# Sublayers begun token tile by token tile, weights in 1024-column units split in place, modulation made one stage ahead, in an eleven-stage transformer kernel

## The reference, cut to what matters

```python
def adaln_sublayer(x, m, f, ln_g, ln_b):          # stages 0 to 5
    shift, scale, gate = m[:, None, 0], m[:, None, 1], m[:, None, 2]
    y = f(x * (1 + scale) + shift)
    return layer_norm(DEEPNORM_ALPHA * x + (1 + gate) * y, ln_g, ln_b)

mod = silu(c) @ mod_w[layer] + mod_b[layer]       # 2 layers x 9 rows of 1024
# stages 0, 2, 3, 5: f = 0.5 * (silu(u @ w_gate) * (u @ w_up)) @ w_down, inner width 2816
# stage 1: sparse attention and a gated delta rule; stage 4: latent attention (MLA)
# stages 6, 8: x + 0.5 * mixer(rms_norm(x)): two softmax branches and a gated linear
#              attention (GLA), joined by gates
# stages 7, 9: x + (conv over tokens of the up product, gated) @ w_down, of rms_norm(x)
```

## Time and profile before

| | before |
|---|---|
| median of 3 runs | 2538.28 us |
| the profiled execution, its own time | 2538.26 us |
| its span | 2536.5 us |
| PE busy | 2260.5 us (89%) |
| DVE, ACT, POOL busy | 1394.2, 1031.8, 292.5 us |
| chain that ended last | PE 77%, DVE 9%, DMA 5%, ACT 4% |
| moved by DMA | 412.79 MB, mean 163 GB/s |
| granted PE clock, mean | 0.915 |

### The profile page before, as it was taken

The page is one execution under the profiler, slowest core; times in us unless marked ns, Lnnn a source line. Parts: engine busy times, 40 slices in busy tenths (PEclk is TensorE's granted clock), DMA queues, the critical chain, the costliest instruction groups (busy, mean ns, idle before and its releaser), DMA issues.

```text
span 2536.5 us, 34860 instructions
## 1 busy us (share of the span) xinstructions
PE 2260.5 (89%) x14352; PEld 1933.7 (76%) x14352; DVE 1394.2 (55%) x2047; ACT 1031.8 (41%) x1725; POOL 292.5 (12%) x414
## 2 busy tenths in 40 slices
PE   5999889979998998788999588987999778897999
PEld 3998778759986996566998566766998667666997
DVE  3545578664455455366454566335665465445664
ACT  1444353333443443264444343342554333343553
POOL 0000200130002002023000222040000121220000
PEclk8999899989999999798999798858999888858999
DMA  9986432459767874625765343303665433303663
GB/s 318 267 237 230 136 113 95 133 159 300 197 225 226 241 223 159 216 76 162 193 194 191 105 134 100 116 17 109 164 185 191 123 126 91 133 10 107 188 184 137
DMA packets 442750, 412.79 MB, mean 163 GB/s; under 512 B 22034, under 2 KB 387814, under 8 KB 442464
## 3 DMA queue, kind: packets, MB, share of 16 engines
q1 hardware_dynamic: 435488, 388.80, 50.8%
q0 software_dynamic: 7104, 21.76, 2.9%
HBM read 407.90 MB, written 2.62 MB: 162 GB/s over the span
## 4 chain that ended last, share of the span: by engine, by line
PE 77%; DVE 9%; DMA 5%; ACT 4%; issue 2%; POOL 2%; SPq 0%; DVEq 0%; ACTq 0%; POOLq 0%
PE ps L170 74%; PE ps L173 3%; DVE arena L179 2%; DMA arena<-in_mod_w 2%; DVE wlo L179 2%; ACT whi L176 2%; ACT arena L176 1%; DMA raw<-in_ffn_w_up 1%; DVE tmp L179 1%; DVE arena L191 1%; DMA raw<-in_mla_w_q_up 1%; POOL arena L221 1%; POOL tmp L179 1%; DVE small L197 1%; DVE ul L179 0%
## 5 line engine op out<-in xcount | busy, mean ns | idle before, releaser
L179 DVE TENSOR_TENSOR wlo<-raw,whi 128x1024 fp32r<-128x1024 f32 (+2 forms) x594 | 728.8, 1231 | 737.3 <-ACT whi L176 736.9
L176 ACT ACTIVATE whi<-raw 128x1024 fp32r<-128x1024 f32 (+2 forms) x594 | 608.3, 1043 | 463.9 <-PE ps L170 408.6
L170 PE MATMUL ps<-uh,whi 128*128 128x256 f32 x2392 | 694.5, 290 | 23.5 <-DVE mb L191 8.1
L170 PE MATMUL ps<-ul,whi 128*128 128x256 f32 x2392 | 685.9, 287 | 0.0
L170 PE MATMUL ps<-uh,wlo 128*128 128x256 f32 x2392 | 685.5, 287 | 0.0
L170 PEld LDWEIGHTS ps<-uh,whi 128*128 128x128 f32 x2392 | 468.9, 196 | 44.7 <-issue 21.1
L170 PEld LDWEIGHTS ps<-ul,whi 128*128 128x128 f32 x2392 | 468.9, 196 | 0.3 <-issue 0.2
L170 PEld LDWEIGHTS ps<-uh,wlo 128*128 128x128 f32 x2392 | 468.3, 196 | 0.0
L170 PE MATMUL ps<-whi,arena_r 128*128 128x512 f32 x1184 | 367.0, 390 | 0.0
L170 PE MATMUL ps<-whi,uh 128*128 128x512 f32 (+3 forms) x594 | 251.3, 423 | 72.6 <-ACT arena L176 28.5
L170 PE MATMUL ps<-arena 128*128 128x128 f32 (+8 forms) x1360 | 262.5, 341 | 28.4 <-DVE tmp L191 10.8
(11 more groups left out here) (179 smaller groups left out, 1794.7 us busy)
## 6 DMA issues: line engine op xcount, KB each, us to landing
arena<-in_mod_w SPq DMA_DIRECT2D x64, 1024.0 KB, 7.1
raw<-in_ffn_w_gate SPq DMA_DIRECT2D x88, 512.0 KB, 6.6
raw<-in_ffn_w_up SPq DMA_DIRECT2D x88, 512.0 KB, 6.9
raw<-in_ffn_w_down SPq DMA_DIRECT2D x44, 1024.0 KB, 5.0
raw<-in_w_in SPq DMA_DIRECT2D x44, 1024.0 KB, 5.2
raw<-in_w_up SPq DMA_DIRECT2D x88, 512.0 KB, 5.1
raw<-in_w_down SPq DMA_DIRECT2D x22, 1024.0 KB, 4.9
raw<-in_hyb_w_in SPq DMA_DIRECT2D x16, 1024.0 KB, 5.3
```

The lines of the kernel that those rows point to most:

```text
L170: return Nothing() if self.raw is None else self.raw.matmul(out, l, r, start=start, stop=stop)
L176: return Nothing() if self.raw is None else self.raw.activation(out, src, func, **kw)
L179: return Nothing() if self.raw is None else self.raw.tensor_tensor(out, a, b, op)
```

## The change

It has five parts. (1) Weights: a ring of eight units of 128 x 1024 (0.5 MB); the low part is written over `raw`, so a place is free only when PE has used the unit (`sp_units` waits for `used`). The low part of `wlo` has no place of its own any more. (2) FFN: PE takes blocks (c, t): 256 columns of gate and 256 of up beside each other, the weights moving with 512 columns and u of one token tile stationary. The result stands with tokens on partitions and is transposed by two matmuls for each block (`pe_ffn_turn`). The first blocks are (0,0), (1,0), (0,1), (1,1). (3) Stages 1, 4, 6 and 8 begin with one or two 512-column products by token tile (`pe_tok_halves`): z in stage 1, c0 in stage 4, gv and t1a in the mixers, which stood later in the stage before. (4) The boundary is done for t = 0 first, in halves of 512 columns, and for t = 1 under the first products of the next stage. (5) Modulation groups belong to the stage ahead: none at the boundary but two products where an FFN follows; twelve in an FFN's blocks, in the rest of stage 1, or between the attention units of stage 4 instead of its projections. `LATE` is 4.

```diff
+def sp_units(sp, M, n=1):
+    for u in range(sp.unit, min(sp.unit + n, len(M.units))):
+        if u >= NUNIT:                      # 8
+            sp.wait_ge(*sp.on("used", u - NUNIT))
...
+def pe_tok_halves(pe, M, jobs, ready, between):
+    for t in range(T):
+        for tag, src, c0, c1, banks, emptied in jobs:
...
+            for uid, v in units[tag]:
+                pe.wait_ge(*pe.on("lo", uid))
+                for i in range(v.hi.shape[1]):
+                    pe.each(*ready(t, k))
...
+        if t == 0:
+            between()                       # transposes u of t = 1
...
+MOD_BLOCKS = (2, 4, 5, 7, 9, 10, 12, 14, 15, 17, 19, 20)
+UNITS_AFTER = [0, 0, 2, 4] + [2] * (2 * NC - 4)
 def pe_ffn(...):
+    for j, (c, t) in enumerate(FFN_ORDER):
+        if j == 2:
+            second_half()
+        if j > 1:
+            pe_mod_sum(pe, M, 3)
...
+        for uid, v in units[c]:
+            pe.wait_ge(*pe.on("lo", uid))
+            for r in range(2):
+                pe.each(*ready(t, k))
+                last = mm3(pe, bank, M.uT[:, k, t * P:(t + 1) * P], v[:, r, :], k == 0, k == KD - 1)
...
+        for i in TURNS_AFTER[j]:
+            pe_ffn_turn(pe, M, n, i)
+        if j in MOD_BLOCKS:
+            pe_mod(pe, M, 7)
...
 def dve_out(dve, M, n):
+    dve_norm(dve, M, n, 0)
+    dve_into(dve, M, n, 0, m)
+    dve_turn_in(dve, M, n, 0, U_BANKS[0])
...
+    dve_unit(dve, M, LATE // 2)
+    dve_norm(dve, M, n, 1)
+    dve_unit(dve, M, LATE - LATE // 2)
+    dve_into(dve, M, n, 1, m)
+    dve_turn_in(dve, M, n, 1, U_BANKS[1])
...
 def pool_out(pool, M, n):
+    for t in range(T):
+        pool_rstd(pool, M, n, t)
+    pool_bias(pool, M, 3 * n + 5)
+    pool.wait_ge(*pool.on("ln_v", "u", n, 1, 1))
...
 def pool_mixer_loads(pool, M, n):
-    pool.wait_ge(*pool.on("x_dve", n - 1, 1))
+    pool.each(made(pool, M, ("s", n - 1), 1))     # last product of both tiles
...
 def act_program(act, M):
+    act_unit(act, M, NUNIT)
+    for t in range(T):
+        act_turn_in(act, M, -1, t, U_BANKS[t])
     act_positions(act, M)
...
 def pool_program(pool, M):
+    pool_rms_gain(pool, M, 6, A["attn_norm_2"][0], pool.on("ln_v", "u", 4, 1, 1))
+    pool_rel(pool, M)
+    pool_mixer_loads(pool, M, 6)
+    pool_next(pool, M, 5)
...
 def sp_program(sp, M):
-            sp_mods_open(sp, M, inner_groups(n), *u_ready(sp, n - 1))
-            sp_chunk(sp, M, NSLOT)
...
+            sp_mods_open(sp, M, n, sp.on("flip", "mkT", 7))
```

More of the change, by code:

```diff
@@ L298, in area_two @@
                      for i in range(2)))
[L304 to L319, removed]
@@ L322, in raw_view @@
[L322 to L330, removed]
-def unit_view(M, u):
[L334 to L340, removed]
@@ L343, in sp_chunk @@
[L343 to L352, removed]
@@ L355, in act_unit, with pe_units @@
-def act_unit(act, M, n=1):
[L357 to L362, removed]
-def dve_unit(dve, M, n=1):
[L367 to L371, removed]
+def pe_units(pe, M, a, b, axis, *pieces):
+    whole, per = (a, UNIT // b) if axis == "a" else (b, UNIT // a)
+    out = []
+    for i in range(0, whole, per):
+        j = min(whole, i + per)
+        if axis == "a":
+            parts, shape = [(src[:, i:j, :], c0, c1) for src, c0, c1 in pieces], (j - i, b)
+        else:
+            parts, shape = [(src[:, :, max(i, c0) - c0:min(j, c1) - c0], max(i, c0) - i, min(j, c1) - i)
+                            for src, c0, c1 in pieces if c0 < j and c1 > i], (a, j - i)
+        out.append(pe_unit(pe, M, shape, parts, True))
+    return out
@@ new lines, in pe_unit, with raw_view @@
+def pe_unit(pe, M, shape, parts, split):
+    u = pe.unit
+    pe.unit += 1
+    if u == len(M.units):
+        M.units.append(dict(shape=shape, parts=parts, split=split))
+    return u, (unit_view(M, u) if split else raw_view(M, u))
+def raw_view(M, u):
+    a, b = M.units[u]["shape"]
+    return M.raw[:, u % NUNIT, 0:a * b].rearrange("p (a b) -> p a b", a=a)
+def unit_view(M, u):
+    a, b = M.units[u]["shape"]
+    return Two(*(x[:, u % NUNIT, 0:a * b].rearrange("p (a b) -> p a b", a=a) for x in (M.whi, M.wlo)))
@@ new lines, in landed @@
+def landed(e, M, u):
+    return e.on(f"ring{u % NUNIT}", u, len(M.units[u]["parts"]) - 1)
+def sp_units(sp, M, n=1):
+    for u in range(sp.unit, min(sp.unit + n, len(M.units))):
+        if u >= NUNIT:
+            sp.wait_ge(*sp.on("used", u - NUNIT))
+        raw, k = raw_view(M, u), M.units[u]
+        for i, part in enumerate(k["parts"]):
+            dst = raw[:, :, part[1]:part[2]] if k["split"] else raw[64 * i:64 * i + 64]
+            sp.dma(dst, part[0]).then_inc(*sp.dv(f"ring{u % NUNIT}", u, i))
+        sp.unit = u + 1
@@ new lines, in act_unit @@
+def act_unit(act, M, n=1):
+    while n and act.unit < len(M.units):
+        u = act.unit
+        act.unit += 1
+        if M.units[u]["split"]:
+            act.wait_ge(*landed(act, M, u))
+            act.activation(unit_view(M, u).hi, raw_view(M, u), ACT.Copy).then_inc(*act.ev("hi", u))
+        n -= 1
+def dve_unit(dve, M, n=1):
+    while n and dve.unit < len(M.units):
+        u = dve.unit
+        dve.unit += 1
+        if M.units[u]["split"]:
+            v = unit_view(M, u)
+            dve.wait_ge(*dve.on("hi", u))
+            dve.tt(v.lo, raw_view(M, u), v.hi.bitcast(F32), ALU.subtract).then_inc(*dve.ev("lo", u))
+        n -= 1
@@ L433, in pe_tok @@
     pe.each(*ready)
[L434 to L438, removed]
[L439 to L450 removed]
+    k = 0
@@ L461, in tok_units @@
 def tok_units(e, M, nk, w, unit):
-    n = sum(len(rows) for rows in tok_chunks(nk, w))
+    n = len(tok_rows(nk, w))
     for i in range(n):
```

1016 lines of the change are left out of this document (511 added, 505 removed).

## The result

| | before | after |
|---|---|---|
| median | 2537.50 us (4 runs) | 2861.31 us (4 runs, 2856.84 to 2877.79) |
| ratio after / before | | 1.129, 95% interval 1.124 to 1.134 |
| profiled execution, its span | 2538.26, 2536.5 us | 2864.90, 2862.8 us |

The change made the kernel 324 us slower, where 2509 us and a range up to 2550 were forecast. First the page of the kernel after, parts 1, 2, 4, 5 and 6.

What follows compares the result with a forecast made beforehand. It took PE's own queue, busy nine tenths of the span, plus its pauses as the bound. Terms -27 + 25 + 25 - 24 + 7.5 - 13 + 3 - 14 - 12 + 2 - 1 = -28.5 from 2538.3 gave 2509 us, range 2468 to 2550.

Steps and rivals of the forecast that it cites:

- rival (b): FFNs: SP held, so PE starves; 2.5 us in each of 34 blocks, +85 us, 2594 us; chance 0.13.
- Rival (c): All weights in 0.5 MB loads: transfers bound by their number, +155 us in four FFNs, about 2660 us; chance 0.03.
- FFN width: Gate and up in four FFNs: 528 matmuls of 512 columns replace 1056 of 256, -27 us.
- transposes: FFN blocks: two added transposes of h per block, 0.28 us a pair, +25 us for four FFNs.
- sums: FFN modulation: PE waits for ACT's copy before 34 sums, 0.74 us each, +25 us.
- a boundary: Boundaries 1 to 2, 2 to 3, 4 to 5: tile by tile order saves 8 us each, -24 us.
- E: Moment tile 0's last product is done at a boundary; the next stage's first product was forecast at about E + 11 us.
- The start: Kernel start: eight units stand ahead of u's split on ACT while mod_w loads, +2 us, bounds -5 to +10.
- Stage 1 with its boundary: Boundary 0 to 1 and stage 1, z moved to the front: +1.5 and +6 us, bounds -5 to +15.
- Stage 4: Twelve modulation groups move from projections (-23 us) to attention (+9 us): -14 us, bounds -28 to +5.
- The mixers: Stages 6 and 8: t1a at the front saves 6 us each; boundaries 5 to 6 and 7 to 8 save 6 and 7.
- Stages 7 and 9: Boundaries 6 to 7 and 8 to 9: delay with no gain of its size, +3 us for both, bounds -6 to +8.

Runs made afterwards that it cites:

- e1: Changed kernel with the third and fourth modulation loads of FFNs having two boundary products issued ahead of the FFN's blocks: 2721.55 us.
- e2: Changed kernel with ACT and DVE splitting units three places behind the newest load in stages 1, 4, 6 and 8: 2705.55 us.
- e12: e5 with split two behind, denser stage 1 modulation groups, and two catch-up units placed behind the result's transposes in stages 1 and 4: 2480.36 us, ratio 0.979.
- e3: Changed kernel with both the early modulation loads of e1 and the split three units behind of e2: 2561.64 us.
- e6: e5 without its sum edit, so FFN modulation sums stand in front of the next block as in the changed kernel: 2511.24 us.
- e5: e3 plus four edits: start order on ACT, later FFN modulation sums, POOL's small loads behind the root, both x updates first before stages 7 and 9: 2491.06 us.

## Why the prediction was wrong

The step that failed is the argument against rival (b): "eight places cover 21.8 us". It counted how far loads reach ahead of PE, and asked nowhere what stands in front of what in the three queues. So two costs were put at nothing, and the runs give 143 and 159 us for them. A sign of being wrong that the prediction named came: idle time of PE ended by a DMA within the FFN's blocks.

- **Rival (b)**, at 13%, named SP held at a modulation room, 2.5 us in each of 34 blocks, and 2594 us. The place was right, the mechanism reversed: SP was held at the units' `used`, and what came late was the modulation load. In the FFN blocks it was 1.7 to 8.1 us, 20 times, all in stages 2, 3 and 5, where two groups had gone to the boundary (e1: 143 us). Units hardly starved: outside the start PE waited 5.6 us in all for a unit's low part. The prediction said itself that the modulation loads stand in the same in-order queue as the units', but did not follow that order through a block.
- **The split at the newest unit** has no term in the sum at all (e2: 159 us). I listed it only as a load's time from issue to use, as if only PE waited. DVE and ACT wait too, and the chain's next step is behind them.
- **The clock** has no term. Of the 20 pauses in stages 2, 3 and 5 the three of 1.7 to 2.0 us left PE at the upper level; the other 17 were followed by matmuls at the lower one (e1: 143 us for 108 us of pauses). The prediction also read the earlier trace rows too kindly: the row has two sevens and two fives, not eights and one five.
- **Rival (c)**: the runs decide against it. With every weight still in loads of 0.5 or 0.25 MB, e12 is faster than before. A load of `w_in` landed 3.6 us after issue (1 MB: 5.2 before).

With the two causes removed, e3 measures the rest of the sum: +23 us against -28.5 forecast, so this rest has the wrong sign too. A part of it is the repair's own price: in stage 1 the units caught up late cost about 3 us (e12). Term by term:

- FFN width, transposes, sums and a boundary together should have made stages 2 and 3 1.2 us shorter each. They are 0.9 and 0.3 shorter, and stage 5 is 3.4 shorter, not 7. Wide matmuls stand 0.227 apart within a block, 12 ns less than two of 256 columns, where 13 were forecast. The exposed copy was 0.66 us for each of 31 sums, and 20.2 us in all (e6), where 25 was forecast.
- At boundary 2 to 3, E is 890.2 by PE's queue (24 held matmuls of 0.227 us end at 895.7). The first product came at 900.54, E + 10.3. The prediction wrote E + 11, but its own terms add up to 10.2. Behind it PE waited 1.61 us for a unit's low part and 1.41 us for tile 1's split, where one pause of up to 6 us was forecast. This boundary was modelled well. DVE's norm and PE:

```profile
890.73 1.22 DVE L177 TENSOR_TENSOR tmp<-ps,mb 128x1024 f32<-128x1024 f32 x1
```
```profile
900.54 0.47 PE L168 MATMUL ps<-whi,uh 128*128 128x512 f32 x1 [0.24 <-DVE ul L177]
```

- The start was forecast at +2, and by the first FFN product it is +2.6: 55.73 against 53.17. That hides the same mistake in small: ACT's eight units stand ahead of tile 0's u and each waits for its load, and e5's order alone brought that product forward by 9.2 us. Eight modulation products stand ahead of it in both kernels, not twelve as the prediction has it. Stage 0 is +17.7 against +10.3 by the prediction's terms; two pauses in its first blocks, 0.98 us for `ul` and 3.55 us for DVE's gating, have no term. Stage 1 with its boundary is +12.2 against +7.5. The first product before the change:

```profile
53.17 0.55 PE L170 MATMUL ps<-uh,whi 128*128 128x256 f32 x1 [2.98 <-DVE wlo L179]
```

- Stage 4 gave 7.6 of 14. The prediction took no pause of 10 us at its start as a sign of being right; in e3 one still stands 47 us into the stage, where the one of 10.91 us stood, now behind DVE:

```profile
1067.24 1.12 PE L171 MATMUL ps<-con,arena 128*128 128x128 f32 x4 [9.98 <-DVE arena L189]
```

- The mixers: +1.0 and -5.1 in e3, where -12 and -13 were forecast. Their boundaries gave 9.9 and 7.3 us up to the first product of u, no less than forecast; the rest of the two stages grew by 10.9 and 2.2 us, where t1a was to give 6 in each. Why is open. In the changed kernel's chain at 5 to 6 the small loads stand ahead of the root, as forecast, 6.84 us:

```profile
1613.60 6.84 POOL arena L219 x13
...
1620.52 0.19 POOL small L184
```

- Stages 7 and 9, +5.4 and +4.1 against +1.5 each: they need both tiles, so tile by tile only delays them. In e3, PE pauses twice (e5 took 6.8 and 7.0 us out):

```profile
1791.44 1.94 PE L171 MATMUL ps<-con,tmp 128*128 128x128 f32 x8 [3.30 <-DVE tmp L189]
1802.37 1.94 PE L171 MATMUL ps<-con,tmp 128*128 128x128 f32 x8 [8.99 <-DVE tmp L189]
```

## What to carry to other kernels

A ring has two distances: how far loads run ahead of the consumer, and how far the in-order engine that prepares a unit stays behind the newest load. If the second is nothing, each step of whatever else that engine does waits for a full load; here three units of slack were worth 159 us, and two did as well as three. When work is moved from inside a loop to its front, move the loads that belong to it by as many steps, or each arrives a fixed distance late through the whole loop. And ask of each engine that would wait, not only of the busiest, what is queued behind it.

## What the runs showed of the hardware

- A pause of PE of 6.65 us was followed by matmuls at the lower of the two clock levels: 0.43 us between matmuls of 512 columns, where 0.227 is usual, and 1.93 us for a modulation product in place of 1.07. Behind a pause of 1.69 us the same product took 1.07. Removing 108 us of pauses gave 143 us.
- A matmul of 512 columns costs 0.227 us and one of 256 columns 0.1196, not half of it, at the upper clock level. At the lower level they stand 0.427 and 0.213 us apart, two to one.
- A load of 0.5 MB landed 3.6 us after issue at the median in the mixers. With unit loads issued right behind it, the 1 MB load of `mod_w` at 626.63 took 8.60, where 3.0 us lie between landings of 1 MB loads at the kernel's start.
